# One shared gate/up block and half-height down products at the end of the first four FFNs

## What is computed

```
D_FF = 2752
def swiglu(h, w1, w3, w2):
    return (jax.nn.silu(h @ w1) * (h @ w3)) @ w2
for l in range(DEPTH):                      # first block, DEPTH = 2
    x = x + 0.5 * m[:, 0, 2][:, None] * swiglu(adaln_in(x, ...), ffn_w1[l, 0], ffn_w3[l, 0], ffn_w2[l, 0])
    ...                                     # mixer
    x = x + 0.5 * m[:, 2, 2][:, None] * swiglu(adaln_in(x, ...), ffn_w1[l, 1], ffn_w3[l, 1], ffn_w2[l, 1])
D_FF_2 = 2816                               # second block
```

## Time and profile before

| | |
|---|---|
| median of 3 runs | 2054.28 us (2052.86 to 2058.66) |
| the profiled execution | 2054.2 us, its span 2052.4 us, clock 0.961 |
| PE busy | 1896.0 us (92% of the span) |
| DVE busy | 1430.1 us (70%) |
| ACT busy | 991.6 us (48%) |
| chain that ended last | PE 71%, DVE 15%, ACT 6%, DMA 5% |

### The profile page before, as it was taken

How to read it: one execution, slowest core, us unless ns; L and a number is a source line. 1 busy time by engine, 2 the same in 40 slices (tenths; PEclk the granted TensorE clock), 3 DMA queues, 4 the chain that set the end, 5 groups by cost and what they waited for, 6 DMA issues and landing times.

```text
span 2052.4 us, 38258 instructions
## 1 busy us (share of the span) xinstructions
PE 1896.0 (92%) x16490; PEld 1628.8 (79%) x16490; DVE 1430.1 (70%) x2238; ACT 991.6 (48%) x1596; POOL 6.5 (0%) x14
## 2 busy tenths in 40 slices
PE   3999988999999999999999989599999999879997
PEld 2888766888788876788888878368888888758887
DVE  6889675878798887666686665645666766656664
ACT  3444654544544555444554453235546544555543
POOL 0000000000000000000000000000000000000000
PEclk7999998999999999999999999599999999989999
DMA  8989533677599833465655545004654555423551
GB/s 328 382 347 359 212 134 125 256 270 265 203 358 361 328 124 124 155 247 218 232 186 204 197 180 191 31 4 173 225 190 180 216 203 198 155 93 124 216 191 78
DMA packets 54277, 424.00 MB, mean 207 GB/s; under 512 B 5955, under 2 KB 6131, under 8 KB 26683
## 3 DMA queue, kind: packets, MB, share of 16 engines
q1 hardware_dynamic: 52172, 413.59, 53.5%
q0 software_dynamic: 1936, 7.95, 1.1%
HBM read 420.38 MB, written 1.13 MB: 205 GB/s over the span
## 4 chain that ended last, share of the span: by engine, by line
PE 71%; DVE 15%; ACT 6%; DMA 5%; issue 2%; SPq 0%; DVEq 0%; ACTq 0%
PE pw L405 14%; PE pw L407 14%; PE pw L406 14%; PE acc L405 8%; PE acc L407 8%; PE acc L406 8%; DVE ring_lo L1519 6%; DMA land<-stream 4%; ACT ring_hi L1100 2%; DVE modw L1414 1%; DMA modw<-wmod 1%; PE pssq L473 1%; PE pw L595 1%; PE pw L592 1%; PE acc L627 1%
## 5 line engine op out<-in xcount | busy, mean ns | idle before, releaser
L405 PE MATMUL pw<-h_hi,ring_hi 128*128 128x256 bf16 x3248 | 891.7, 275 | 50.2 <-DVE h_lo L1505 36.5
L406 PE MATMUL pw<-h_lo,ring_hi 128*128 128x256 bf16 x3248 | 891.7, 275 | 0.0
L407 PE MATMUL pw<-h_hi,ring_lo 128*128 128x256 bf16 x3248 | 891.5, 274 | 0.0
L1519 DVE TENSOR_TENSOR ring_lo<-land,ring_hi 128x1024 bf16<-128x1024 f32 x633 | 738.2, 1219 | 177.8 <-ACT ring_hi L1100 177.4
L1100 ACT ACTIVATE ring_hi<-land 128x1024 bf16<-128x1024 f32 x633 | 623.2, 1045 | 235.7 <-PE acc L407 121.7
L405 PEld LDWEIGHTS pw<-h_hi,ring_hi 128*128 128x128 bf16 x3248 | 318.4, 98 | 114.3 <-issue 49.2
L405 PE MATMUL acc<-a_hi,ring_hi 128*128 128x256 bf16 x1408 | 383.9, 273 | 2.4 <-DVE a_lo L1569 2.4
L406 PE MATMUL acc<-a_lo,ring_hi 128*128 128x256 bf16 x1408 | 383.9, 273 | 0.0
L407 PE MATMUL acc<-a_hi,ring_lo 128*128 128x256 bf16 x1408 | 383.9, 273 | 0.0
L407 PEld LDWEIGHTS pw<-h_hi,ring_lo 128*128 128x128 bf16 x3248 | 319.7, 98 | 39.7
L406 PEld LDWEIGHTS pw<-h_lo,ring_hi 128*128 128x128 bf16 x3248 | 318.7, 98 | 38.3 <-issue 0.3
(11 more groups left out here) (259 smaller groups left out, 1530.0 us busy)
## 6 DMA issues: line engine op xcount, KB each, us to landing
land<-stream SPq DMA_DIRECT2D x211, 1536.0 KB, 6.5
modw<-wmod SPq DMA_DIRECT2D x144, 512.0 KB, 7.7
biasT<-bias_rows POOLq DMA_DIRECT2D x3, 1536.0 KB, 8.6
biasT<-bias_rows POOLq DMA_DIRECT2D x1, 3072.0 KB, 14.5
cst_s<-cst SPq DMA_DIRECT2D x1, 1792.0 KB, 10.0
x<-xT SPq DMA_DIRECT2D x1, 1024.0 KB, 9.7
out<-proj SPq DMA_DIRECT2D x1, 1024.0 KB, 3.9
par_s<-par SPq DMA_DIRECT2D x1, 699.0 KB, 13.4
```

The source lines that it names most:

```text
L405: mm(o, lhs[0], rhs[0], start=start, stop=False, skip_group_check=True)
L406: mm(o, lhs[0], rhs[1], start=False, stop=False, skip_group_check=True)
L407: return mm(o, lhs[1], rhs[0], start=False, stop=stop, skip_group_check=True)
L1519: v.tensor_tensor(ring_lo[:, t % RING, b, :], land[:, t % LAND, b, :], ring_hi[:, t % RING, b, :], ALU.subtract).then_inc(lo_ready, 1)
```

## The change

In the first four FFNs (i < 6) the last step has 64 units, not 128.

- The host packs the last 64 gate columns and the last 64 up columns into block 0 of the last triple. Block 1 of it stays zeros; it is still transferred and split.
- `up(21)` is one run of 24 matmuls and not two. Its result has the gate values on partitions 0 to 63 and the up values on 64 to 127 of the same 256 columns of pw.
- Silu, multiply, copy and subtraction of step 21 cover 64 partitions. The multiply reads its gate values from partitions 0 to 63 and its up values from PSUM's partitions 64 to 127.
- `down(21)` contracts 64 rows: the weights and the hidden units of its 24 matmuls are cut to partitions 0 to 63.

```diff
+        def rows(i, j):
+            return P // 2 if i < 6 and j == NFF - 1 else P
...
-                    for b in range(2):
+                    for b in range(2 if rows(i, j) == P else 1):
...
-                    m = product(accv[:, k, :], weights(t0 + j, 2, k, slice(0, P)),
-                                [a_hi[:, j % (LAG + 1), :], a_lo[:, j % (LAG + 1), :]],
+                    w = rows(i, j)
+                    m = product(accv[:, k, :], [half[0:w] for half in weights(t0 + j, 2, k, slice(0, P))],
+                                [a_hi[0:w, j % (LAG + 1), :], a_lo[0:w, j % (LAG + 1), :]],
...
-                    fn(sig[:, j % 2, :], pw[j % (LAG + 1)][:, 0:S], ACT.Silu).then_inc(silu_done, 1)
+                    fn(sig[0:rows(i, j), j % 2, :], pw[j % (LAG + 1)][0:rows(i, j), 0:S], ACT.Silu).then_inc(silu_done, 1)
...
-                    up_half = act_in[:, j % 2, :] if deferred(i) else pw[j % (LAG + 1)][:, S:2 * S]
-                    v.tensor_tensor(act_in[:, j % 2, :], sig[:, j % 2, :], up_half, ALU.mult).then_inc(gated_ready, 1)
+                    w = rows(i, j)
+                    up_half = act_in[:, j % 2, :] if deferred(i) else pw[j % (LAG + 1)][:, S:2 * S] if w == P else pw[j % (LAG + 1)][w:P, 0:S]
+                    v.tensor_tensor(act_in[0:w, j % 2, :], sig[0:w, j % 2, :], up_half, ALU.mult).then_inc(gated_ready, 1)
...
         for b, w in enumerate((w1, w3)):
-            full = np.zeros((D, FPAD), f)
-            full[:, :w.shape[1]] = w
-            blocks[t:t + NFF, b] = tiles(full)
+            whole = w.shape[1] // P
+            blocks[t:t + whole, b] = tiles(w[:, :whole * P])
+        if whole < NFF:
+            blocks[t + whole, 0] = tiles(np.concatenate([w1[:, whole * P:], w3[:, whole * P:]], axis=1))[0]
```

More of the change, by code:

```diff
@@ L1107, in silu @@
                     act.wait_ge(gu_ready, f * NFF + j + 1)
-                    fn(sig[:, j % 2, :], pw[j % (LAG + 1)][:, 0:S], ACT.Silu).then_inc(silu_done, 1)
+                    fn(sig[0:rows(i, j), j % 2, :], pw[j % (LAG + 1)][0:rows(i, j), 0:S], ACT.Silu).then_inc(silu_done, 1)
                 act.wait_ge(gated_ready, f * NFF + j + 1)
-                fn(a_hi[:, j % (LAG + 1), :], act_in[:, j % 2, :], ACT.Copy).then_inc(a_hi_ready, 1)
+                fn(a_hi[0:rows(i, j), j % (LAG + 1), :], act_in[0:rows(i, j), j % 2, :], ACT.Copy).then_inc(a_hi_ready, 1)
                 if j < NFF - 1 and (j or not deferred(i)):
@@ L1565, in gated @@
                         dve.wait_ge(triple_used, t0 + j - LAG)
-                    up_half = act_in[:, j % 2, :] if deferred(i) else pw[j % (LAG + 1)][:, S:2 * S]
-                    v.tensor_tensor(act_in[:, j % 2, :], sig[:, j % 2, :], up_half, ALU.mult).then_inc(gated_ready, 1)
+                    w = rows(i, j)
+                    up_half = act_in[:, j % 2, :] if deferred(i) else pw[j % (LAG + 1)][:, S:2 * S] if w == P else pw[j % (LAG + 1)][w:P, 0:S]
+                    v.tensor_tensor(act_in[0:w, j % 2, :], sig[0:w, j % 2, :], up_half, ALU.mult).then_inc(gated_ready, 1)
                     dve.wait_ge(a_hi_ready, f0 + j + 1)
-                    v.tensor_tensor(a_lo[:, j % (LAG + 1), :], act_in[:, j % 2, :], a_hi[:, j % (LAG + 1), :], ALU.subtract).then_inc(act_ready, 1)
+                    v.tensor_tensor(a_lo[0:w, j % (LAG + 1), :], act_in[0:w, j % 2, :], a_hi[0:w, j % (LAG + 1), :], ALU.subtract).then_inc(act_ready, 1)
                     if i == 2 and j in LAYER_AT:
```

## The result

The changed kernel takes 2067.32 us (median of 6 runs, 2061.14 to 2073.86); the kernel before, run beside it, 2054.65 us (2052.86 to 2058.66). The ratio is 1.0057, with a 95% interval of 1.0040 to 1.0074: slower by 0.57%, more than the 0.3% that can be told from no change, and outside the range of 2050.0 to 2058.8.

The account below looks back on a forecast made before the run. TensorE looked first, but VectorE was nearly as late at the four FFN ends; 4.2 us of gains less 2.1 for changes of height and 1.7 for the clock gave -0.4: 2053.8 us, range 2050.0 to 2058.8.

Parts of the forecast that it names:

- What is late next: Ends of FFN 1 to 4: down(21) waits for VectorE's a_lo; gains 0, 2.0, 0.5, 1.7, together 4.2 of 10.5 us.
- The rival that all 96 matmuls come off: FFN 1 to 4: TensorE sets the end everywhere, 10.5 us gained, 2043.7 us; chance 0.04.
- The changes of height: Rounds after down(19): seven switches between 128-row and 64-row weights, 0.10 us each, 0.7 us per FFN, 2.1 us in FFN 1 to 3.
- The slower rival: down(21)'s 24 products per FFN: loads of successive 64-row weights not hidden, 2.4 us per FFN, together +7.6, 2061.8 us; chance 0.07.
- The clock: Behind FFN 1's new 3.8 us idle time: 3.3 us of work at half speed, costing 1.7 us; nothing in FFN 3.
- The upper bound of 4.6 us: FFN 1: the most the clock's fall could cost, all 42 remaining matmuls at half speed, 42 x 0.109 us.
- The sum: Net of gains and additions: FFN 1 +2.4, FFN 2 -1.3, FFN 3 +0.2, FFN 4 -1.7, together -0.4 us.
- FFN 3's new 2.1 us: TensorE's idle time ahead of down(21) in FFN 3, taken as too short to lower the clock, so no cost.
- The row of 2.7 us at 802.2: Profile row of PE from which the prediction took that the clock stays at 1.00 after 2.7 us of idle time.
- The rival of a longer fall: Clock low beyond 3.3 us in FFN 1, or also in FFN 3: up to 4.6 us each, 2056 to 2059; beyond 0.3%, chance 0.02.

Follow-up runs that it names:

- another kernel with the same end: The changed kernel with FFN 3 as before, so FFN 1, 2 and 4 keep the change: 2061.50 us, ratio 1.0033 to the kernel before.
- the kernels with single FFNs: The change limited to some FFNs, against the kernel before: FFN 1, 2, 4 ratio 1.0033; FFN 2, 4 ratio 0.9989; FFN 3 ratio 1.0030.
- the probe: The kernel before, with FFN 3's gate and up products of steps 0 to 2 contracting only 64 rows: 2075.19 us, ratio 1.0102.
- half height, nothing else: The kernel before with activations and down(21) on 64 partitions, up(21) still 48 matmuls from two blocks: 2056.93 us, ratio 1.0009.

## Why the prediction was wrong, point by point

**What is late next: right.** The waits of TensorE for a_lo stand at all four ends with the lengths that were worked out, and VectorE's rows at FFN 1 and FFN 3 are as before. The rival that all 96 matmuls come off is out.

**The changes of height: right in size.** At the end of FFN 2, at full clock, the starts in the timeline of PE are 0.109 us apart within a run and 0.20 and 0.21 us from run to run, 0.09 to 0.10 more:

```profile
527.54 0.27 PE L410 MATMUL acc<-a_lo,ring_hi 64*128 64x256 bf16 x1
527.65 0.27 PE L411 MATMUL acc<-a_hi,ring_lo 64*128 64x256 bf16 x1
527.85 0.28 PE L409 MATMUL acc<-a_hi,ring_hi 128*128 128x256 bf16 x1
...
528.41 0.27 PE L411 MATMUL acc<-a_hi,ring_lo 128*128 128x256 bf16 x1
528.62 0.28 PE L409 MATMUL acc<-a_hi,ring_hi 64*128 64x256 bf16 x1
528.74 0.27 PE L410 MATMUL acc<-a_lo,ring_hi 64*128 64x256 bf16 x1
```

**The slower rival: the right sign by the wrong mechanism.** Loads of 64-row weights are hidden within a run, by the same rows. The rule of the Trainium skill that it rested on, "TensorE: Matmul & The Clock Gate", Part 3 (Packing small matmuls), that a load overlaps only where the row group is another, does not hold for these runs: same rows 0 to 63, bfloat16, starts 0.11 us apart.

**The clock: the step that failed, in two ways.** First, its price. I wrote "If it brings the same 3.3 us at half speed, the matmuls behind it lose 1.7 us", from a stretch in which full-height float32 products followed. In FFN 3 the clock was low for 13.7 us in both traces of the changed kernel, and in FFN 1 for 3.4 us in one of them, not at all in the other, and for 17.1 us in the trace of another kernel with the same end. The sum had +2.4 us for FFN 1 and +0.2 for FFN 3; the kernels with single FFNs give +9 and +6. The upper bound of 4.6 us, "all 42 remaining matmuls at half speed", was no bound: the first 3.9 us of the sums of squares behind them ran at half speed too. What the runs put in its place: half-height products alone did not bring the clock back (the probe, 31 us), and half-height and full-height ones in turn did so late in six of the seven falls, after 10.2 to 17.1 us. I had priced the new operation's duration and its loads, and taken for granted that it counts as work for the clock. Second, its place. "FFN 3's new 2.1 us is below the shorter one: nothing." It was 2.37 us, and the clock fell at its end. The row of 2.7 us at 802.2 showed one idle time of that length without a fall; one row is not a limit. The idle times also vary: FFN 1 had 3.70, 1.72 and 5.89 us in three traces with the same instructions there, FFN 3 2.37, 3.58 and 2.14. They hang on when a transfer lands. Ahead of step 20 of FFN 1 VectorE's split waits for ScalarE's for 1.04 us in the first of these traces and 1.33 in the third and not in the second, and in all three ScalarE's split waits for the transfer. The kernel before varies at this place as well, 1.17 us in its trace and 3.80 in that of the probe, which has the same instructions up to FFN 3. The prediction used one execution's.

**The rival of a longer fall** was the right direction, at 2056 to 2059 us and with a chance of 0.02 beyond 0.3%. It should have been the main question. The change makes TensorE idle and then gives it half-height work, at the two ends where VectorE is latest.

**What stays open.** In the first trace FFN 1's half-height rounds followed 3.70 us of idle time and the clock was low for 3.4 us only; nothing here tells this case from the long ones. Nor is it shown when the clock falls at all. With half-height rounds behind it, an idle time of 2.14 us (FFN 3 alone changed) was followed by a fall and one of 2.66 us (half height, nothing else) was not. With full-height rounds, one of 2.92 us was and one of 3.38 us was not. The length of the idle time alone does not order these. The runs at 2068 us and above have no trace; that they have long falls at both ends fits the sum of the single FFNs, and is not shown.

## What to carry to other kernels

Taking work from the engine that bounds a kernel pays only where the next engine has room, so read the last wait of each place before adding up what comes off. On TensorE ask of shortened work not only how long it takes but what the clock does with it: zeros contracted at full height were cheaper here than half the rows, behind an idle time. Where work comes off ahead of a wait, move other work in front of that wait in the same edit.

## What the runs showed of the hardware

- Matmuls of 64 rows and 128 x 256 results, back to back for 31 us, left the granted clock at 0.50 from the idle time of 4.55 us ahead of them until 4.7 us after full-height products had begun. Full-height products behind the same idle time had it back after 6 us of work.
- Seven low stretches began at an FFN's end with half-height work behind it in the traces here: 13.7 us three times, 10.2 twice, 17.1 and 3.4 once each. The five with full-height work behind it had 3.4 us (four) and 6.8 us (one). The part of a stretch that lies in the idle time is included.
- Half-height rounds behind 0.2 to 1.72 us of idle time left the clock at 1.00, and so did those behind 2.66 us in one trace.
- A change between 64-row and 128-row weights costs 0.09 to 0.10 us in bfloat16 at the full clock, in either direction.
- VectorE's multiply with its two inputs on different partitions (0 to 63 and 64 to 127) takes 0.42 us, as the one with both on the same takes 0.41.
